# One encoder step on one NeuronCore: start order, FFN norms, two weight-split orders and end sums rearranged

## What is computed

```python
for i in range(DEPTH):                       # 2
    xn = rmsnorm(x, g_mix[i])
    if i % N_MIXERS == 0:
        y, (C, n, m) = mlstm_mixer(xn, ...)  # xn @ a_w_in -> q, k, v, o, gates; scan over chunks; @ a_w_out
    else:
        y, v = chunk_mlp_mixer(xn, ...)      # gelu(xn @ b_w_in) -> u, v; layernorm(v); (u * (mix v + b)) @ b_w_out
    x = x + y
    x = x + swiglu(rmsnorm(x, g_ffn[i]), f_w_gu[i], f_w_down[i])   # (silu(g) * up) @ w_down, width 2816
y = rmsnorm(x, g_final)
```

## Time and profile before

| | us |
|---|---|
| median of 3 runs | 2819.62 |
| lowest and highest of them | 2817.20, 2824.18 |
| the profiled execution | 2816.03 |
| its span in the trace | 2814.0 |
| TensorE busy / weight loads busy | 2766.8 / 2719.6 |
| VectorE, ScalarE, GpSimd busy | 1529.3, 748.8, 1110.4 |

### The profile page before, as it was taken

The page is one execution under the profiler, slowest core; times in us unless marked ns, Lnnn a source line. Parts: engine busy times, 40 slices in busy tenths (PEclk is TensorE's granted clock), DMA queues, the critical chain, the costliest instruction groups (busy, mean ns, idle before and its releaser), DMA issues.

```text
span 2814.0 us, 48597 instructions
## 1 busy us (share of the span) xinstructions
PE 2766.8 (98%) x18454; PEld 2719.6 (97%) x18454; DVE 1529.3 (54%) x2886; ACT 748.8 (27%) x1481; POOL 1110.4 (39%) x731
## 2 busy tenths in 40 slices
PE   7999999999999999999999999999999999999999
PEld 6999999999999999999999999999999999999998
DVE  4454452697555555556611465710475555555556
ACT  5203030452222222222411311300432222222224
POOL 3232322225444444444243133443244444444441
PEclk9999999999999999999999999999999999999999
DMA  3322222211111111111111111111111111111112
GB/s 106 72 79 48 71 43 67 48 37 47 45 45 45 45 45 45 45 45 46 37 46 38 44 57 45 46 39 39 44 37 46 45 45 45 45 45 45 45 45 86
DMA packets 188212, 139.45 MB, mean 50 GB/s; under 512 B 6899, under 2 KB 176715, under 8 KB 188108
## 3 DMA queue, kind: packets, MB, share of 16 engines
q1 hardware_dynamic: 188108, 137.96, 17.1%
HBM read 127.32 MB, written 10.62 MB: 49 GB/s over the span
## 4 chain that ended last, share of the span: by engine, by line
PE 88%; DVE 8%; ACT 2%; issue 1%; SPq 0%; DMA 0%; POOL 0%; ACTq 0%; DVEq 0%; POOLq 0%
PE ps L1223 32%; PE ps L883 23%; PE ps L1268 18%; PE ps L1341 7%; PE ps L1048 3%; PE ps L1401 1%; DVE xn_lo L1996 1%; DVE xs_lo L2351 1%; DVE xs_lo L2003 1%; PE ps L1447 1%; PE ps L1158 1%; PE ps L1164 0%; PE ps L1160 0%; PE ps L1138 0%; DVE xT L2334 0%
## 5 line engine op out<-in xcount | busy, mean ns | idle before, releaser
L1223 PE MATMUL ps<-xs_hi,w_lo 128*128 128x288 f32 x2496 | 743.9, 298 | 0.0
L1223 PE MATMUL ps<-xs_hi,w_hi 128*128 128x288 f32 x2496 | 739.0, 296 | 4.1 <-DVE hidden L2307 2.3
L1223 PE MATMUL ps<-xs_lo,w_hi 128*128 128x288 f32 x2496 | 738.5, 296 | 0.0
L811 POOL TENSOR_TENSOR w_lo<-w_raw,w_hi 128x512 fp32r<-128x512 f32 x304 | 402.0, 1324 | 582.0 <-ACT w_hi L1629 582.0
L787 POOL TENSOR_TENSOR w_hi<-w_raw,ones 128x1024 fp32r<-128x1024 f32 x80 | 193.4, 2418 | 798.1 <-PE ps L883 614.2
L1223 PEld LDWEIGHTS ps<-xs_hi,w_hi 128*128 128x128 f32 x2496 | 469.2, 188 | 6.7 <-DVE hidden L2307 2.8
L1223 PEld LDWEIGHTS ps<-xs_lo,w_hi 128*128 128x128 f32 x2496 | 471.3, 189 | 0.3
L1223 PEld LDWEIGHTS ps<-xs_hi,w_lo 128*128 128x128 f32 x2496 | 469.0, 188 | 0.0
L1629 ACT ACTIVATE w_hi<-w_raw 128x512 fp32r<-128x512 f32 x304 | 189.8, 628 | 783.5 <-POOL w_raw L837 243.7
L2334 DVE TENSOR_TENSOR xT<-xT,ps 128x384 f32<-128x384 f32 x528 | 286.7, 551 | 194.5 <-PE ps L1268 186.8
L1268 PE MATMUL ps<-hg_hi,w_hi 128*128 128x384 f32 x1008 | 339.0, 336 | 3.6 <-DVE hg_lo L2326 2.9
(11 more groups left out here) (328 smaller groups left out, 4978.9 us busy)
## 6 DMA issues: line engine op xcount, KB each, us to landing
w_raw<-in_f_w_gu_dram SPq DMA_DIRECT2D x88, 512.0 KB, 3.9
w_raw<-in_f_w_down_dram SPq DMA_DIRECT2D x44, 512.0 KB, 3.7
w_raw<-in_b_w_in_dram SPq DMA_DIRECT2D x32, 512.0 KB, 4.0
w_raw<-in_a_w_in_dram SPq DMA_DIRECT2D x24, 512.0 KB, 4.3
w_raw<-in_b_w_out_dram SPq DMA_DIRECT2D x16, 512.0 KB, 4.2
out_dram<-y_out SPq DMA_DIRECT2D x9, 512.0 KB
x_in<-in_x_prompt_dram SPq DMA_DIRECT2D x8, 512.0 KB, 6.2
c_nat<-in_state_C_dram SPq DMA_DIRECT2D x8, 512.0 KB, 8.7
```

The lines of the kernel that those rows point to most:

```text
L811: nc.gpsimd.tensor_tensor(left(layer, w_lo, pos), src, left(layer, w_hi, pos).bitcast(F32), ALU.subtract).then_inc(left_lo, 1)
L1223: ins = pe.matmul(out, left(layer, w, pos)[:, k, :], r[:, s, x, k, :], start=(first and k == 0 and m == 0), stop=(last_one and k == KH - 1 ...
```

## The change

Six things at once. (1) Start: `gate_piece(0)` moves ahead of tile 6, the two first query pieces ahead of the row matmuls, and ScalarE squares tiles 2 to 8 only after all copies; the gate steps move to later places (`gates_turn` behind the first key piece, the rest into the v pass); head 0 of ScalarE and of GpSimd is written out. GpSimd's unit 1 now waits until VectorE's low parts are through. (2) For tile 0 of each head the product with the zero state is left out. (3) FFN norms: TensorE sums over rows (one column a tile), ScalarE roots and VectorE inverts [128, 9], VectorE writes the factors on diagonals and TensorE spreads them; T4 moves behind the last `hidden_lo`. (4) Chunk MLP: 12 of the 24 low parts move behind the additions, the first group's sums between the additions 15 to 17, the row sums out of the way of tile 7, tile 8 last; its norm by rows too. (5) The last gate units go (2,0), (2,1), (3,0), (3,1), (2,2), (3,2), and GpSimd's third unit of `b_w_out` waits for 42 low parts. (6) End: the first group's squares one addition earlier, its row sums and turns one piece later.

```diff
-GATE_BANKS = [3, 4, 5]
-ROW_BANKS = [2, 6, 7]
+IN_BANK = list(range(8)) + [0, 1, 2, 3] + [4, 6, 7, 3, 1, 2]
+GATE_BANKS = [5, 3, 4]
+ROW_PARTS = [(5, 384, 8, 1), (6, 0, 0, 3), (6, 384, 6, 1), (7, 0, 3, 3), (7, 384, 7, 1)]
+GATE_STEPS = [(0, 0, 2), (0, 0, 3), (0, 0, 4), (0, 1, 0), (1, 0, 7)]
...
-U_PIECES_LAST = U_PIECES[:6] + [(u, g) for g in range(NG) for u in (2, 3)]
+U_PIECES_LAST = U_PIECES[:6] + [(2, 0), (2, 1), (3, 0), (3, 1), (2, 2), (3, 2)]
...
+LOWS_WITH = {**{m: m - 1 for m in range(1, 9)}, **{m: m - 3 for m in range(11, 15)}}
+SUMS_WITH = {15: 0, 16: 1, 17: 2}
-TURN_AFTER = {15: 0, 17: 1, 19: 2, 22: 3}
+TURN_AFTER = {16: 0, 18: 1, 20: 2, 22: 3}
-ROWS_AFTER = {13: 0, 22: 1}
+ROWS_AFTER = {14: 0, 22: 1}
...
@@ gpsimd
-            with pool.Fori(0, H) as h:
+            for u in range(8):
+                split_unit(W_HEADS, 0, u, (n_lo, KD * NG) if u == 1 else None)
+            with pool.Fori(1, H) as h:
...
+            split_unit(W_BO, 0, 0)
+            split_unit(W_BO, 0, 1, (used, W_BO.count(0, 1, 1 + FREE_UNITS - 3)))
+            pool.wait_ge(ps_lo, len(P_ORDER) - 6)
+            split_unit(W_BO, 0, 2)
+            split_unit(W_BO, 0, 3)
+            with pool.Fori(1, KD // 2) as i:
...
@@ tensor, start
+                if c == 2 * TPG:
+                    pe.wait_ge(split, 1)
+                    turned_in(GATE_BANKS[0], 2 * c)
+                    gate_piece(0)
...
-            pe.wait_ge(xt_dve, NT)
-            pe.wait_ge(xt_act, NT)
-            for g in (1, 2):
-                gate_piece(g)
+            first_query(0)
+            turned_in(GATE_BANKS[1])
+            gate_piece(1)
+            first_query(1)
+            turned_in(GATE_BANKS[2])
+            gate_piece(2)
             pe.wait_ge(row_diag, 1)
...
@@ tensor, heads
-                    pe.matmul(bank(t, DV + 1), dmat[:, c, :], v_tok[:, c, :], start=True, stop=False)
-                    if c < NP:
+                    ins = pe.matmul(bank(t, DV + 1), dmat[:, c, :], v_tok[:, c, :], start=True, stop=(c == 0))
+                    if 0 < c < NP:
...
@@ tensor, ffn
-                    if at == 5:
-                        sum_first(0)
-                        sum_first(1)
-                    if at == 6:
-                        sum_first(2)
-                    if b > 4:
-                        pe.wait_ge(r_root, NG * (n - 1) + 8 - b)
+                    if at == 4:
+                        rows_first(0)
+                    elif at == 5:
+                        bank_free(5)
+                        spread_first(0)
+                        pe.wait_ge(f_root, 2 * layer + 1)
+                    elif at == 6:
+                        pe.wait_ge(f_norm, N_SPREAD * layer + 2)
+                    elif at == 7:
+                        rows_first(1)
                     first_piece(0, c, q)
+                spread_first(1)
...
@@ tensor, chunk MLP, v group 0
-                    v_half(group, V_ROUNDS[1][0:2], 0)
-                    pe.wait_ge(d_add[0], N_DOWN * N_FFN + 8)
-                    row_sums(2, 7)
-                    v_half(group, V_ROUNDS[1][2:], 0)
+                    v_half(group, [5, 6], 0)
+                    row_sums()
+                    v_half(group, [7], 0)
+                    v_half(group, [5, 6, 7], 1)
+                    v_half(group, [8], 0)
+                    v_half(group, [8], 1, 8)
...
@@ vector, ffn
+                def inverse(part):
+                    c0, c1 = F_PARTS[part][0], F_PARTS[part][-1] + 1
+                    dve.wait_ge(f_root, 2 * layer + part + 1)
+                    dve.reciprocal(r_tok[:, c0:c1], r_tok[:, c0:c1]).then_inc(f_inverse, 1)
...
                 lows(2)
+                inverse(0)
                 lows(3)
                 add_up(n, 2)
-                for g in range(NG):
-                    dve.wait_ge(r_root, NG * (n - 1) + g + 1)
-                    dve.reciprocal(tok(rstd_f[:, :], g), tok(rstd_f[:, :], g)).then_inc(r_ready, 1)
...
-                for s in range(2):
-                    gained_minus(s, X_T4, 1, 0, X_T2)
                 for at, (c, q) in enumerate(FIRST_UP[4:], 4):
                     hidden_lo(0, at - 1, FIRST_UP[at - 1][1] // 2, first_bank(*FIRST_UP[at - 1]) % 4)
                     dve.wait_ge(first_mm, 16 * layer + 8 + at + 1)
                     hidden(0, at, q // 2, first_bank(c, q) % 4)
                 hidden_lo(0, 7, FIRST_UP[7][1] // 2, first_bank(*FIRST_UP[7]) % 4)
+                for s in range(2):
+                    gained_minus(s, X_T4, 1, 0, X_T2)
                 for m in range(N_DOWN):
                     add_down(0, m)
...
@@ vector, last down pass of layer 0
-                        if before_mixer and m > 0:
-                            lower(2, G_MIX + KD, *BY_GROUP[m - 1])
+                        if before_mixer and m in LOWS_WITH:
+                            lower(2, G_MIX + KD, *BY_GROUP[LOWS_WITH[m]])
+                        if before_mixer and m in SUMS_WITH:
+                            add_up(2, 0, [SUMS_WITH[m]])
```

More of the change, by code:

```diff
@@ L923, in gate_piece, with turned_in, first_query @@
                 ins.then_inc(gt_mm, 1)
+            def turned_in(b, t=2 * NT):
+                n = in_before(b, t)
+                pe.wait_ge(xt_act if n % 2 else xt_dve, n // 2 + 1)
+            def first_query(g):
+                pe.wait_ge(split, W_HEADS.count(0, 0, 1))
+                turned_in(g)
+                unit_piece(W_HEADS, 0, g, g, None, g == NG - 1).then_inc(a_mm, 1)
             pe.wait_ge(const_ok, 1)
@@ L1088, in head @@
                     unit_piece(W_HEADS, 4, g, HEAD_O_BANK + g).then_inc(a_mm, 1)
+                    if first and g < 2:
+                        turn(g + 1)
                 def wait_bank(t):
@@ L1240, in first_piece, with rows_first, spread_first @@
                     ins.then_inc(first_mm, 1)
-                def sum_first(g):
-                    pe.wait_ge(summed, NG * (n - 1) + g + 1)
-                    pe.matmul(bank(7 - g), ones[:, :], tok(rstd_f[:, :], g), start=True, stop=True).then_inc(r_sum, 1)
+                def rows_first(part):
+                    b, at = F_ROWS_AT[part]
+                    for c in F_PARTS[part]:
+                        pe.wait_ge(summed, NG * (n - 1) + c // TPG + 1)
+                        c0 = at + c - F_PARTS[part][0]
+                        ins = pe.matmul(ps[b][:, c0:c0 + 1], rstd_f[:, c * P:(c + 1) * P], ones[:, 0:1],
+                                        start=True, stop=True)
+                    ins.then_inc(f_rows, 1)
+                def spread_first(part):
+                    pe.wait_ge(f_turned, 2 * layer + part + 1)
+                    for b, at, c, count in F_SPREAD[part]:
+                        pe.matmul(ps[b][:, at:at + count * P], ones[:, :], f_diag[:, c:c + count, :],
+                                  start=True, stop=True).then_inc(f_spread, 1)
                 def down(i, first):
@@ L1527, in row_squares @@
                 act.activation(sq_junk[c % 2], x_in[:, c, :], ACT.Square, accum_out=r_v[:, c:c + 1]).then_inc(x_squared, 1)
-            for g, ahead, after in ((0, (0, 1), ()), (1, (), (2, 3, 4)), (2, (), (5, 6))):
-                for c in ahead:
-                    row_squares(c)
+            for g in range(NG):
+                if g == 0:
+                    row_squares(0)
+                    row_squares(1)
                 for c in range(g * TPG, (g + 1) * TPG):
@@ L1622, in _ @@
                     act.activation(tok(sig_o[:, 1, :], g), bank(t), ACT.Sigmoid).then_inc(t_act, 1)
+            head(0)
+            with act.Fori(1, H) as h:
+                head(h)
             def ffn(layer, n, gain, added, free):
@@ L1760, in ffn @@
                         act.activation(t1, t1, ACT.Copy, scale=gains[:, gain + k:gain + k + 1]).then_inc(x_t1, 1)
+                for at in range(4, 8):
+                    gate_first(at)
+                for pos in (8, 9):
+                    round_first(pos, first_mm, 16 * layer + 8)
                 for s in range(2):
@@ L2025, in _ @@
             dve.drain().then_inc(a_fac, 1)
+            for c in range(TPG):
+                turned(c)
+            dve.wait_ge(gains_turned, 1)
+            dve.tensor_copy(gains[:, :], ps[6][:, 0:G_ALL]).then_inc(gains_ready, 1)
+            dve.wait_ge(gains_ready, 1)
             for g in range(NG):
-                turned(g)
+                dve.wait_ge(xt_dve, TPG * (g + 1))
                 for k in range(KD):
                     lower(0, G_MIX, g, k)
+                    if g < NG - 1 and k in TURN_WITH[g]:
+                        turned(TPG * (g + 1) + TURN_WITH[g].index(k))
             dve.wait_ge(x_root, 1)
```

263 lines of the change are left out of this document (144 added, 119 removed).

## The result

Median 2814.93 us over 15 runs (2808.46 to 2820.25) against 2819.62 (2812.07 to 2829.34) over 15 of the kernel before: ratio 0.9977, 95% interval 0.9967 to 0.9988. By the ratio the change is 6.5 us faster, between 3.4 and 9.3; the two medians lie 4.7 apart. The forecast was 2801.7, 17.9 faster, with a range that ended at 2811; as a whole it was right in the sign alone. The profiled execution has a span of 2809.2 against 2814.0, 4.8 less. A behind a view or a number names the rows of the kernel before that it is to be held against.

A forecast was written before the change was run, and what follows sets the result against it. TensorE, busy 2766.8 of 2814 us, was taken as the bound, leaving idle time and lowered clock to gain. Terms -5.2 - 1.7 + 3.0 - 8.0 - 4.3 - 1.7 = -17.9 gave a median of 2801.7 us, range 2790 to 2811.

The forecast's parts named there:

- Start: Reordered start through head 0: 12.8 us gained, 7.6 lost again in head 0, together -5.2 us.
- 6.0 plus one fall: Head 0, after the o pieces: VectorE operations slowed beside GpSimd cost 6.0 us, plus 1.6 for one clock fall.
- rival that head 0 keeps what it gains: GpSimd is through before VectorE's operations, or the store is issued earlier: 7.6 us less, 2794.1; chance 0.25.
- Zero state: Tile 0 of each head: a pair of half-matmuls with `state` occupies 0.43 us; four heads give -1.7 us.
- In the other heads nothing but 0.43 us each: Heads other than head 0: the profile would show no change except the 0.43 us saved in each.
- FFN norms: Both FFN starts: -0.6 us for earlier up pieces, +2.0 for low parts, +1.6 for clock; +3.0, bounds -3.5 and +6.
- for the clock one fall in two such waits, 1.6: Waits of 2 to 3.3 us after the first down passes, one a layer: one clock fall between them, 1.6 us.
- Chunk MLP: Before the chunk MLP, to the end of v group 0: -8.0 us, with half a chance of one fall; bounds -9 and -5.
- low parts beside GpSimd's splits give place to additions: VectorE before the chunk MLP: low parts of 2.3 us beside splits, 0.6 otherwise, move; last sum at 1371.4.
- Gate units and output product: Last gate units and output product: the 1.3 us and 3.0 us waits go, -4.3 us, bounds -2.5 and -4.3.
- released some 9 us before its use: Output product: GpSimd's third unit, waiting for 42 low parts, is still released some 9 us before it is needed.
- End: Kernel's end: first group's sums 1.04 us earlier, row sums one piece later; -1.7 us, bounds -0.8 and -1.8.

The follow-up runs named there:

- before_shift8: The kernel before, with sixteen fulfilled TensorE waits (eight instructions) ahead of the loop over heads 1 to 3; 2821.35 us, one run.
- loads_early: The changed kernel, with SyncE issuing head 0's loads of units 5 and 6 ahead of its wait for the gate rows; ratio to the kernel before 0.9949.
- bv_hold: The changed kernel, with GpSimd's third unit of the chunk MLP's v weights held until VectorE's last row of squares is added up; ratio to the kernel before 0.9968.
- bo_36: The changed kernel, with GpSimd's third unit of b_w_out released at 36 low parts instead of 42; ratio to the kernel before 0.9977.
- t4_back: The changed kernel, with T4 back at its old place, ahead of the fourth `hidden_lo`, in both layers; ratio to the kernel before 0.9952.

## Why the prediction was wrong, and where it was right

The measured terms fall short of the forecast by 13.1 us in the traces: 3.8 in the loop's place, 2.3 at the FFN starts, 2.1 before the chunk MLP, 4.3 at the output product, and 0.6 in small ones.

- **Start, right, its size with some luck.** "Without a gap to the last key piece", v pass end "near 89" (90.5), unit 5 "at about 102.5" (104.0), "6.0 plus one fall" (5.97, and a granted clock of 0.69 from 113.86 to 120.00): head 0 ends 5.5 us earlier against 5.6. Both traces carry chance: the start of the kernel before ended 5.8 us sooner in `before_shift8`. The rival that head 0 keeps what it gains was put on the right cause: `loads_early` is that case.
- **Zero state, right**, 0.43 us a head (11.01 to 10.58), but covered up by what follows.
- **Missing term: the loop's place, +3.8.** "In the other heads nothing but 0.43 us each" failed. The "issue" waits stood in the list before (3.2 us in all) and I left them out as not touched. Instructions added ahead of a loop were counted as free.
- **FFN norms, right in mechanism, mis-sized by 2.3.** The wait at `x_los`, forecast at 2 to 3.3 us, is 3.2. T4 ended 4.9 us behind the up pieces (5.0), the additions and low parts took 23.0 us (22.3; five of the eight low parts long, not four), the restart came at 28.2 (27.4). The term that failed is "for the clock one fall in two such waits, 1.6": it fell behind both, for 2.6 and 1.4 us, 4.0 in all (passes of 47.7 and 46.4 us against 45.06). Behind the same 3.2 us wait it fell 15 times in the 20 that ten traces hold, so one in two was too low a chance.
- **Chunk MLP, mis-sized by 2.1.** "The last sum at 1371.4" came at 1372.4, the row sums waited 1.34 instead of 0.9, and the clock fell. The step "low parts beside GpSimd's splits give place to additions" missed that twelve low parts and two additions of the first sum still stood beside the splits; `bv_hold` gave back 3.0, which puts the stage at -8.9, my bound.
- **Gate units and output product, wrong, 4.3.** The old waits went, as forecast. But "released some 9 us before its use" was wrong twice: it was released 5.6 us before (1820.51 to 1826.11), and I had priced contention only as VectorE waiting for GpSimd. It was GpSimd that waited, 2.6 us, and TensorE for it, 2.06. That wait is the step that failed: it took half of the 4.3. What was left of the gain went to something that no step of the sum had, the 3.4 us of slower pace behind it at a granted clock of 1.00 (1008 matmuls in 178.3 us against 174.9 in `bo_36`). In the traces without the slower pace the stage is 3.4 shorter than before, inside my bounds.
- **End, nearly right**: -1.4 for -1.7; 0.64 us waits for an addition (L2438) before the first turn.
- **Clock, counted too low.** I priced two and a half falls at 1.6 us. In the changed kernel's trace it fell behind five of the seven gaps of 1.3 us and more that follow the start: those of 5.97, 1.81, 3.23, 1.34 and 3.22 us, not those of 2.09 and 2.06. Behind one and the same gap it fell in one kernel's execution and not in another's: after the 2.07 us wait of `bo_36` the output product ran at 1.00, after the 2.05 us of `loads_early` at 0.99, and 1008 matmuls took 179.8 us, of which 3.4 are the slower pace.

## What to carry to other kernels

When a transfer or a unit is moved, look at who shares a path with the engine that takes it up, in both directions: the one that runs already shuts the other out, and a closely packed row of operations does so until its end, so a wait that merely releases the other engine earlier buys nothing. Operations that are moved off one path belong into their engine's idle moments, not at the head of its next chain without slack. Look at the gaps called "issue" behind a long loop's return, and try the loop at another place in the program before judging a change of 0.3%. And do not settle a term of a few us from one trace each: look at the same stage in every trace whose program is the same there.

## What was not expected of the hardware

- The place of a loop of about 1,660 instructions decides over 4 to 12 us in two returns. TensorE's other loops, of 1,021 instructions and fewer, show no such gap. What is fetched, and why 2015 and 2031 are good and 1995 to 2011 bad, no run here shows. That the gaps are instruction fetches was argued, not shown; that the place alone makes them is shown.
- TensorE has two paces at a granted clock of 1.00: 24 matmuls of 384 columns take 4.16 or 4.24 us. Each pace was held evenly for 40 such pieces and more, and the traces that differ in it ran the same program there. Steady FFN passes (gate, up and down, 480 matmuls) show the same: 69.76 us in both layers of the changed kernel, 70.13 in layer 0 of `t4_back`, 70.24 in layer 1 of `bo_36`, pass after pass. That is 3.4 us in an output product and 3.4 to 4.3 us an FFN layer by no visible wait, and of the size of the spread of single runs. Its cause was not tried.
